# Up-projection loop: each TensorE product of 512 columns becomes two of 256

## What is computed

```python
def conv_ffn(h, w_up, w_conv, b_conv, w_down):
    u = causal_dwconv(h @ w_up, w_conv) + b_conv
    a, b = jnp.split(u, 2, axis=-1)
    return (jax.nn.gelu(a, approximate=True) * b) @ w_down
```

## Time and profile before

| | us |
|---|---|
| median of 3 runs | 2180.85 (2180.1 to 2181.74) |
| the execution that was profiled | 2181.64 |
| its span, from first to last instruction | 2179.9 |
| loop of the up-projection in it, 84 chunks | about 460 (1471.0 to 1931.1) |

### The profile page before, as it was taken

One profiled execution on the slowest core, in us unless ns is written; L12 is line 12 of the kernel. 1 busy time (PEld: TensorE's weight loads), 2 busy tenths in 40 slices (PEclk: granted clock), 3 DMA queues, 4 the chain that ended last, 5 costly groups with the idle time before them and its releaser, 6 DMA issues.

```text
span 2179.9 us, 33196 instructions
## 1 busy us (share of the span) xinstructions
PE 2152.4 (99%) x12606; PEld 1830.6 (84%) x12606; DVE 1434.1 (66%) x1651; ACT 1065.1 (49%) x1438; POOL 246.5 (11%) x220
## 2 busy tenths in 40 slices
PE   7999999999999999999999999989999999999998
PEld 6888888788888888888888888878888888888887
DVE  6986658677654546467765544578778777876444
ACT  6452245446444444445444444566656665644443
POOL 1133000000000101025110001412111111100000
PEclk9999999999999999999999999999999999999999
DMA  7543344445665665676556643636556555656664
GB/s 265 176 149 114 119 149 153 137 152 185 194 191 192 190 195 189 194 263 189 186 191 193 191 149 113 204 118 206 193 185 197 193 191 183 199 188 213 192 193 152
DMA packets 107072, 393.85 MB, mean 181 GB/s; under 512 B 11888, under 2 KB 12144, under 8 KB 106576
## 3 DMA queue, kind: packets, MB, share of 16 engines
q1 hardware_dynamic: 106672, 391.10, 55.7%
q10 hardware_dynamic: 288, 1.18, 0.2%
HBM read 390.14 MB, written 2.10 MB: 180 GB/s over the span
## 4 chain that ended last, share of the span: by engine, by line
PE 92%; DVE 5%; ACT 2%; issue 1%; DMA 1%; SPq 0%; DVEq 0%; ACTq 0%
PE bank L1019 24%; PE bank L1028 12%; PE bank L554 6%; PE sm L441 5%; PE sm L440 5%; PE sm L438 5%; PE bank L1231 3%; PE bank L1233 3%; PE bank L1232 3%; PE bank L557 3%; PE bank L438 2%; PE bank L440 2%; PE bank L441 2%; PE sm L606 2%; DVE part L1987 1%; PE bank L1115 1%
## 5 line engine op out<-in xcount | busy, mean ns | idle before, releaser
L1987 DVE TENSOR_TENSOR part<-part,part 128x1024 fp32r<-128x1024 f32 x724 | 929.4, 1287 | 542.2 <-ACT part L1284 532.4
L1284 ACT ACTIVATE part<-part 128x1024 fp32r<-128x1024 f32 x724 | 764.0, 1058 | 598.9 <-PE sm L441 177.6
L1019 PE MATMUL bank<-part,part 128*128 128x512 f32 x2336 | 563.5, 392 | 0.1
L1019 PEld LDWEIGHTS bank<-part,part 128*128 128x128 f32 x2336 | 427.4, 188 | 83.6 <-issue 0.7
L1028 PEld LDWEIGHTS bank<-part,part 128*128 128x128 f32 x2336 | 288.1, 188 | 12.8
L1028 PE MATMUL bank<-part,part 128*128 128x256 f32 x2336 | 290.3, 276 | 0.0
L554 PE MATMUL bank<-part,part 128*128 128x512 f32 x832 | 207.6, 397 | 1.0 <-DVE part L2042 1.0
L438 PE MATMUL sm<-part,part 128*128 128x512 f32 x512 | 199.2, 389 | 0.0
L441 PE MATMUL sm<-part,part 128*128 128x512 f32 x512 | 199.2, 389 | 0.0
L440 PE MATMUL sm<-part,part 128*128 128x512 f32 x512 | 199.2, 389 | 0.0
L554 PEld LDWEIGHTS bank<-part,part 128*128 128x128 f32 x832 | 151.2, 188 | 33.5 <-DVE part L2042 2.2
(11 more groups left out here) (382 smaller groups left out, 2203.7 us busy)
## 6 DMA issues: line engine op xcount, KB each, us to landing
part<-in_w_up SPq DMA_DIRECT2D x176, 512.0 KB, 4.5
part<-in_w_gate SPq DMA_DIRECT2D x128, 512.0 KB, 4.5
part<-in_w_dn SPq DMA_DIRECT2D x88, 512.0 KB, 4.4
part<-in_w_br SPq DMA_DIRECT2D x40, 512.0 KB, 4.5
part<-in_w_out SPq DMA_DIRECT2D x32, 512.0 KB, 4.8
part<-in_w_mk SPq DMA_DIRECT2D x32, 512.0 KB, 4.5
part<-in_w_mv SPq DMA_DIRECT2D x32, 512.0 KB, 4.3
part<-in_w_q SPq DMA_DIRECT2D x32, 512.0 KB, 4.5
```

The source lines that it names most:

```text
L1019: mm = pe.matmul(dst, w[:, 0, k, :], x[:, k0 + k, :], start=start and k == 0, stop=stop and k == n - 1, skip_group_check=True)
L1284: act.activation(parts(m, h)[:, 0, 0:n, :], raw[:, m % 2, h, 0:n, :], cp) .then_inc(sem("hi_done"), 1)
L1987: tt(w[:, 1, 0:n, :], raw[:, m % 2, h, 0:n, :], w[:, 0, 0:n, :].bitcast(f32), SUB).then_inc(sem("lo_done"), 1)
```

## The change

The 14 rounds of the up-projection's loop get a body of their own, `narrow_chunk`. The high weights of one tile are multiplied twice: by the 256 high columns into the bank's left half, then by the 256 low columns into its right half. The order within a chunk becomes high of half 0, low of half 0, high of half 1, low of half 1, for every chunk, so the rotation by m % 3 is gone there. The waits are the same four, each ahead of the group that needs it. `half_used` is raised after the low products of each half. The loop in the output projection and all chunks written out straight keep the old form.

```diff
+            def narrow_chunk(m, at, x):
+
+                pe.wait_ge(prod_out, at(1, m - R_OFF - 1))
+                dst = bank[:, m % 2, :]
+                for h in range(2):
+                    w = parts(m, h)
+                    pe.wait_ge(sem("hi_done"), at(2, 2 * m + h + 1))
+                    for k in range(8):
+                        pe.matmul(dst[:, 0:T], w[:, 0, k, :], x[:, 8 * h + k, 0:T], start=h == 0 and k == 0, stop=False,
+                                  skip_group_check=True)
+                        pe.matmul(dst[:, T:2 * T], w[:, 0, k, :], x[:, 8 * h + k, T:2 * T], start=False, stop=False,
+                                  skip_group_check=True)
+                    pe.wait_ge(lo_done, at(2, 2 * m + h + 1))
+                    for k in range(8):
+                        mm = pe.matmul(dst[:, T:2 * T], w[:, 1, k, :], x[:, 8 * h + k, 0:T], start=False,
+                                       stop=h == 1 and k == 7, skip_group_check=True)
+                    mm.then_inc(half_used, 1)
...
-            loop(M_UP + 4, 14, X1)
+            loop(M_UP + 4, 14, X1, narrow_chunk)
```

More of the change, by code:

```diff
@@ L1077, in two_chunks, with loop @@
                 quarter(m + 1, 3, x).then_inc(half_used, 2)
-            def loop(base, count, x):
+            def loop(base, count, x, one_chunk):
                 with pe.Fori(0, count) as i:
                     for j in range(6):
-                        chunk(base + j, lambda k, v: i * (6 * k) + v, x)
+                        one_chunk(base + j, lambda k, v: i * (6 * k) + v, x)
             def y_norm(value):
@@ L1173, in _ @@
                 chunk(M_WO + j, one, X2)
-            loop(M_WO + 4, 2, X2)
+            loop(M_WO + 4, 2, X2, chunk)
             pe.wait_ge(sem("y_acc"), 33)
```

## The result

The changed kernel takes 2195.68 us (median of 20 runs), the kernel before 2180.86 (median of 20): 14.8 us or 0.68% slower by the medians, forecast 2195.3. The ratio of the means is 1.0052, 95% interval 1.0036 to 1.0069. The kernel before has one kind, 2180.1 to 2183.6.

A forecast was written before the change was run, and what follows sets the result against it. TensorE's product pitch was taken to bound the loop. Long pitch throughout adds 14.5 us to the profiled 2181.64, other terms nothing, giving 2196.1; less 0.8 for the median of runs, 2195.3 us (+0.66%), range 2177.5 to 2200.5.

The forecast's parts named there:

- What bounds the loop: Up-projection loop: TensorE never idles and no other engine is near, so the loop lasts as long as its product pitches sum to.
- The pitches: Loop products of 256 columns take 113.3 ns (short) or 117.7 ns (long); those of 512 take 228.9 ns.
- Which pitch: All narrow products of the loop were taken at the long pitch, 5.650 us a chunk against 5.4755, +14.5 us; chance 0.62.
- the short pitch holds: Rival: long rows of 256s in the loop run at 113.3 ns, 3.1 us less, 2177.8 us; chance 0.15.
- The other reason: Ahead of the loop stand 8 products of 512, not a multiple of three, so long groups of 256s follow.
- From everything else a row falls into the long one.: Rows of 256s reach the short pitch only out of a row of 512s; behind other products or any gap, 117.7 ns.
- Loads: 1344 more loads in the loop, none dropped for a repeated operand; each lies under a product, cost already in the pitch.
- Order and waits: New order in a chunk: one in three wants a high part 0.8 us sooner, reserve 5.1 us; costs nothing.
- What stands behind the loop: The down-projection's 1056 products start in whichever step the loop leaves; put at nothing, within a microsecond or two.
- By turns: Rival: the branch at a round's end resets the step, rounds short or long, 2177.8 to 2195.3 us; chance 0.08.
- Code fetched again: Rival: the loop body, grown from 1.6 to 2.4 packets, is refetched at 13 returns, +39 us, 2234 us; chance 0.09.

The follow-up runs named there:

- split_only: Changed kernel, but with the old order and its rotation kept, so only the high products are split into two of 256; 2195.73 us median, four of ten runs near 2178.
- late9: late8 with the first high product of the first narrow chunk 512 wide, so nine 512s stand ahead of the 256s; 2179.15 us median, ten runs of one kind.
- late8: Changed kernel with the narrow form starting six chunks later, the first six of 84 chunks in the old form; 2195.80 us median of four runs.
- foreign: Changed kernel plus one 64-column product of the identity at the head of each of the 14 rounds; 2198.14 us median of four runs.
- quarter: Changed kernel, but each high product of 512 columns in the loop is four of 128; 2480.62 us in one run.
- order_only: Changed kernel, but high products stay 512 columns wide, in the new order of 8 high, 8 low, 8 high, 8 low; 2184.01 us median of ten runs.

## Why the prediction was right, and where it was not

- **What bounds the loop.** Right. No idle time ahead of any product before or after, and the difference of the loops (14.8 us) is that of the medians (14.8).
- **The pitches.** Right in size: 117.7 forecast, 117.8 measured over 4032; 113.3 forecast, 113 to 113.3 measured in split_only and late9. A row keeps its pitch for thousands of products, where the rows in the loop of before had 16. That was the weakest step, and it held.
- **Which pitch.** Right for 16 runs of 20. My reason was half wrong. I took the gap in the earlier trace rows for the entry of the loop and said that it makes the row long. The gap is a wait for VectorE's addition, and it leaves the kind to chance: seven runs of 30 are short. The rival "the short pitch holds" had 0.15 and came in 0.2 of the runs, near 2177.8 as worked out; I had spoken of it as if one kernel were always the one or the other. So the spread of the times was a part of the result that the forecast did not name. That the median lies on the forecast was in part luck: nothing in the prediction said that the long kind would be the common one, and why it is has not been found. The other reason, eight 512s ahead, would give a long row without the wait (late8).
- **"From everything else a row falls into the long one."** Too wide. It held behind another kind of product (17 places of before; foreign doesn't contradict it), and behind eight 512s in step (late8). Behind nine in step a row is short (late9), and behind a short wait it can be either, so "any gap" was wrong.
- **Loads.** Right that a second load of the same operand is done and not dropped; quarter shows its price of 110 ns, near the 112.5 taken from L524. The Trainium skill's formula for the isolated gap ("TensorE: Matmul & The Clock Gate", section "Back-to-back issue gap") would have given +3.4 us; neither kind has its 109 ns, and the measured pitch decides.
- **Order and waits.** Right that they cost nothing here by themselves: no wait of PE shows in the loop. What they cost lies in the step: order_only is 3.0 us slower than before, and I had put the edit of the order at nothing. In the changed kernel there is no 512 left whose count could matter, so it does not add to the 14.8.
- **What stands behind the loop.** Right. From the first product of the down-projection to the end of the span it is 248.8 us before (1931.11 to 2179.9) and 248.7 now (1944.56 to 2193.3).
- **By turns.** Did not occur in the changed kernel. The 13 returns of the loop leave the step alone.
- **Code fetched again.** Did not occur. The queues of the changed kernel stand below this list, first between 1490 and 1940, then between 1545 and 1940. The one packet of q8 in the first stretch starts at 1496.3, in the loop's first pass, which ends at about 1503.6; the next starts at 1957.2. The prediction had named q8 packets from 1490 on as the sign of this case, without counting the first pass of a longer body. So a body of 2.4 packets is kept over all 13 returns, as one of 1.6 was, whose last packet started at 1487.9. The window of two pages in the Trainium skill ("Runtime: NRT & Kernel Launch", section "Instruction fetch mechanics") does not hold on TensorE here; its 2048 instructions fit what is seen.

```profile
q1 hardware_dynamic: 22979, 83.65, 59.9%
q14 instruction: 4, 0.03, 0.0%
q8 instruction: 1, 0.02, 0.0%
```

```profile
q1 hardware_dynamic: 20159, 73.41, 59.7%
q14 instruction: 1, 0.01, 0.0%
```

## What to carry to other kernels

Splitting a product into two of half the width costs a load more, and 256 columns just cover one (110 against 113 ns); at that width it is the few ns of step between loads and products that decide, and over thousands of products they were 18 us. Where a long row of equal products has two possible pitches, look at what stands right ahead of it: a count of other products sets it once for the whole row, and a wait that is only just late seems to. Take more than one profile, and look at all times and not the median alone; times of two kinds with nothing between are the sign.

## What was not expected of the hardware

- The same instructions ran at 113.3 or 117.8 ns each for 475 us without a change of either, at the same granted clock of 1.00 (851 or 884 products in 100 us). What in the chip makes two stable steps was not found.
- Four 512s between rows turned long into short and short into long, 14 rounds on end; three left long as long. The last 512's own pitch (226, 229 or 232 ns in turn) goes with it: short behind 232, long behind the other two.
- A product of 128 columns cost 110 ns, nearly as much as one of 256: narrowing to 128 gave nothing back (+300 us for the kernel).
